# Token sums of a quartered product: from the head of the product phase into the normalisation loop, in a two-layer decoder step

## What is computed

```
h = rms_norm(x, norm_g[i])            # x: 1056 tokens x 1024
z = h @ W_in                          # 4096 columns (layer 0), 7168 (layer 1)
... pooling (layer 0) or stick-breaking attention (layer 1), memory attention ...
x = x + concat(branch * silu(gate), mem * silu(mgate)) @ w_out
```

## Time and profile before

| | us |
|---|---|
| median of 3 runs | 2482.71 (2480.73 to 2486.89) |
| the profiled execution | 2476.22 |
| its span, first to last instruction | 2474.5 |
| PE busy | 2229.4 (90%) |
| DVE, ACT, POOL busy | 1304.3, 1014.1, 451.2 |
| mean granted TensorE clock | 0.944 of full |

### The profile page before, as it was taken

One profiled execution on the slowest core, in us unless ns is written; L12 is line 12 of the kernel. 1 busy time (PEld: TensorE's weight loads), 2 busy tenths in 40 slices (PEclk: granted clock), 3 DMA queues, 4 the chain that ended last, 5 costly groups with the idle time before them and its releaser, 6 DMA issues. The chain is left out here.

```text
span 2474.5 us, 47020 instructions
## 1 busy us (share of the span) xinstructions
PE 2229.4 (90%) x18709; PEld 1857.7 (75%) x18709; DVE 1304.3 (53%) x2026; ACT 1014.1 (41%) x2096; POOL 451.2 (18%) x541
## 2 busy tenths in 40 slices
PE   4759999995899948999999997769999999997999
PEld 4659988885678738999999997756666666663787
DVE  5474765542531185434444442358888888774311
ACT  4334322222420053433332342336777777775200
POOL 0062321211100043222222220131111111010000
PEclk7879999997999959999999998789999999999999
DMA  5323222205453132333443332668999999987531
GB/s 187 128 66 102 63 74 75 83 20 215 147 169 102 51 119 83 108 105 119 144 130 96 105 104 112 204 238 309 388 409 407 394 396 391 390 313 266 165 102 51
DMA packets 260393, 441.18 MB, mean 178 GB/s; under 512 B 26067, under 2 KB 187295, under 8 KB 260159
## 3 DMA queue, kind: packets, MB, share of 16 engines
q1 hardware_dynamic: 252110, 408.81, 47.1%
q0 software_dynamic: 8064, 29.36, 3.1%
HBM read 367.85 MB, written 70.82 MB: 177 GB/s over the span
## 5 line engine op out<-in xcount | busy, mean ns | idle before, releaser
L232 DVE TENSOR_TENSOR h_w_lo<-l_w,h_w_hi 128x512 fp32r<-128x512 f32 x264 | 202.1, 767 | 218.7 <-ACT h_w_hi L225 216.4
L225 ACT ACTIVATE h_w_hi<-l_w 128x512 fp32r<-128x512 f32 x264 | 166.7, 632 | 218.4 <-PE i_c L296 76.0
L191 POOL TENSOR_TENSOR h_w_lo_full<-l_w 128x512 f32<-128x512 f32 x44 | 61.8, 1405 | 620.3 <-DMA l_w<-in_w_in_sb_dram 218.1
L294 PE MATMUL i_x<-h_t_hi,h_w_hi 128*128 128x264 f32 x560 | 162.9, 291 | 7.8 <-ACT i_stage L303 5.7
L294 PE MATMUL i_y<-h_t_hi,h_w_hi 128*128 128x264 f32 x560 | 162.1, 289 | 2.1 <-DVE h_t_lo L246 2.1
L2467 PEld LDWEIGHTS b_krow<-ar_arena,b_qd 128*32 128x32 f32 x3072 | 107.2, 111 | 72.6 <-issue 57.3
L296 PE MATMUL i_x<-h_t_hi,h_w_lo 128*128 128x264 f32 x560 | 160.6, 287 | 0.0
L295 PE MATMUL i_x<-h_t_lo,h_w_hi 128*128 128x264 f32 x560 | 160.0, 286 | 0.0
L295 PE MATMUL i_y<-h_t_lo,h_w_hi 128*128 128x264 f32 x560 | 159.8, 285 | 0.0
L296 PE MATMUL i_y<-h_t_hi,h_w_lo 128*128 128x264 f32 x560 | 159.6, 285 | 0.0
L2467 PE MATMUL b_krow<-ar_arena,b_qd 128*32 128x128 f32 x3072 | 140.7, 279 | 8.0 <-ACT b_kev L2173 6.6
(11 more groups left out here) (337 smaller groups left out, 6512.7 us busy)
## 6 DMA issues: line engine op xcount, KB each, us to landing
ar_arena<-in_cache_sb_k_dram SPq DMA_DIRECT2D x73, 768.0 KB, 9.6
bf_vpage<-in_cache_sb_v_dram SPq DMA_DIRECT2D x64, 768.0 KB, 9.0
b_vpage<-in_cache_sb_v_dram SPq DMA_DIRECT2D x64, 768.0 KB, 8.3
l_w<-in_w_in_sb_dram SPq DMA_DIRECT2D x56, 512.0 KB, 3.9
l_w<-in_cache_sb_k_dram SPq DMA_DIRECT2D x36, 768.0 KB, 9.8
...
```

The costliest lines, as they stand in the source:

```text
L191: gp.tensor_tensor(self.w_full[:, i % RING, :, :], a21, a22, ALU.add).then_inc(self.combined, 1)
L225: act.activation(self.w_hi[:, i % RING, :, :], self.source(i), ACT.Copy).then_inc(self.high, 1)
L232: dve.tensor_tensor(self.w_lo[:, i % RING, :, :], self.source(i), self.w_hi[:, i % RING, :, :].bitcast(F32), ALU.subtract).then_inc(self.r ...
L294: pe.matmul(out, w_hi, t_hi, start=kk == 0 and x in ("P1", "P2", "P5"), stop=False, skip_group_check=True)
```

## The change

The three full-width DVE sums and the one of POOL leave the head of the product phases. In the norm, behind the evacuation of each of tiles 4 to 8, DVE makes that tile's columns of sum 5 (`token_first`), waiting there for ACT's half of the evacuation. POOL makes sums 4, 3 and 6 in the same five column pieces (`token_sums`: 112, 3 x 128 and 32 columns, each 4 deep), in `norm_phase` behind its combines and in `front_phase` ahead of them.

```diff
+    def token_columns(self, t):
+        return slice(max(t * P - HALF, 0), t * P - HALF + (P if t < TILES else SAMPLES))
+
+    def token_first(self, dve, t):
+
+        b11, b12, t1 = (self.full[n][:, :, self.token_columns(t)] for n in (0, 3, 5))
+        dve.tensor_tensor(t1, b12, b11, ALU.subtract).then_inc(self.t_first, 1)
+
+    def token_sums(self, gp):
+
+        cols = [self.token_columns(t) for t in range(4, TILES + 1)]
+        for n, at in enumerate(cols):
+            gp.wait_ge(self.t_first, n + 1)
+            gp.tensor_tensor(self.full[4][:, :, at], self.full[2][:, :, at], self.full[5][:, :, at], ALU.subtract
+                             ).then_inc(self.t_added, 1)
+        for at in cols:
+            gp.tensor_tensor(self.full[3][:, :, at], self.full[2][:, :, at], self.full[3][:, :, at], ALU.subtract
+                             ).then_inc(self.t_added, 1)
+        gp.wait_ge(self.t_added, len(cols))
+        for at in cols:
+            gp.tensor_tensor(self.full[6][:, :, at], self.full[1][:, :, at], self.full[4][:, :, at], ALU.subtract
+                             ).then_inc(self.t_added, 1)
```

```diff
+    def token_high(self, act, t, cols=slice(0, HALF)):
+
+        if t == 5 and cols.start == 0:
+            act.wait_ge(self.t_first, TILES - 3)
+        if t in (4, 3, 6):
+            act.wait_ge(self.t_added, {4: 1, 3: 2, 6: 3}[t] * (TILES - 3))
+        act.activation(self.hi[t][:, :, cols], self.full[t][:, :, cols], ACT.Copy).then_inc(self.t_high, 1)
+
+    def token_rest(self, eng, t, n, signal, cols=slice(0, HALF)):
+
+        eng.wait_ge(self.t_high, n)
+        eng.tensor_tensor(self.lo[t][:, :, cols], self.full[t][:, :, cols], self.hi[t][:, :, cols].bitcast(F32), ALU.subtract
+                          ).then_inc(signal, 1)
+
+    def tokens_scalar(self, act, i):
+
+        if i == 0:
+            for n in range(2):
+                self.token_high(act, 5, slice(n * SUB, (n + 1) * SUB))
+        for t in {0: (0, 1), 1: (4,), 2: (2,), 3: (3,), 4: (6,)}.get(i, ()):
+            self.token_high(act, t)
+
+    def tokens_vector(self, dve, i):
+
+        if i == 0:
+            for n in range(2):
+                self.token_rest(dve, 5, n + 1, self.t_rest, slice(n * SUB, (n + 1) * SUB))
+        for t, n in {0: ((0, 3), (1, 4)), 1: ((4, 5),), 2: ((2, 6),)}.get(i, ()):
+            self.token_rest(dve, t, n, self.t_rest)
+
+    def tokens_gpsimd(self, gp, i):
+
+        for t, n in {3: ((3, 7),), 4: ((6, 8),)}.get(i, ()):
+            self.token_rest(gp, t, n, self.t_rest_g)
...
-        if p == 0:
-            pe.wait_ge(self.t_rest_g if x in ("P3", "P7", "P4") else self.t_rest,
-                       {"P5": 1, "P1": 2, "P2": 3, "P6": 4, "P3": 1, "P7": 2, "P4": 3}[x])
         t = self.TOKENS[x]
         for n in range(2):
+            if p == 0:
+                pe.wait_ge(self.t_rest_g if x in ("P7", "P4") else self.t_rest,
+                           {"P5": n + 1, "P1": 3, "P2": 4, "P6": 5, "P3": 6, "P7": 1, "P4": 2}[x])
```

P5 waits for each half of its operand by itself. The calls, in both product phases (here `pool_phase`, POOL and DVE; ACT has `q.tokens_scalar(act, 0)` and, at the end of its loop, `q.tokens_scalar(act, i + 1)`):

```diff
                 gp.memset(up[:, :, 0:HIST], 0.0).then_inc(s["zeroed"], 1)
-                q.tokens_gpsimd(gp)
                 for j in range(6, AHEAD + 1):
                     q.combine(gp, j)
                 for i, (p, x) in enumerate(q.seq):
+                    q.tokens_gpsimd(gp, i)
                     q.combine(gp, i + AHEAD + 1)
                     for n in range(GROUPS):
                         if (p, x) == (first(n), "P7"):
...
-                q.tokens_vector(dve)
+                q.tokens_vector(dve, 0)
                 for j in range(6, AHEAD):
                     q.remainder(dve, j)
                 for i, (p, x) in enumerate(q.seq):
...
+                    q.tokens_vector(dve, i + 1)
```

`Quads` allocates all seven token tiles at once, ahead of `front_phase`, and there the split memory weights lie in the ring of the token weights (slots 0 to 3 and 4 to 7); the first rounds wait until memory product 6 (`made` 14), and rounds 4 and 5 until product 7 (`made` 16):

```diff
-        w_hi = [k.sb(f"w_hi{n}", [P, KD, WC], F32R) for n in range(2)]
-        w_lo = [k.sb(f"w_lo{n}", [P, KD, WC], F32R) for n in range(2)]
+        w_hi, w_lo = ([ring[:, 4 * n:4 * n + 4, :, :].rearrange("p r k n -> p (r k n)").rearrange("p (k n) -> p k n", n=WC)
+                       for n in range(2)] for ring in (q.w_hi, q.w_lo))
...
-                 8: [("K", 1), ("P", 6), ("W", 7), ("X", 0), ("X", 3), ("P", 7), ("V", 1)]}
+                 8: [("K", 1), ("P", 6), ("W", 7), ("X", 0), ("P", 7), ("V", 1), ("X", 4)]}
...
+                q.token_sums(gp)
+                gp.wait_ge(s["made"], 14)
                 for j in range(6):
                     q.combine(gp, j)
...
-                            for j in range(n, n + 3):
+                            act.wait_ge(s["made"], 16 if n else 14)
+                            for j in range(n, min(n + 4, 6)):
                                 q.round(act, j)
```

More of the change, by code:

```diff
@@ L105, in __init__ @@
         self.full, self.lo = [], []
-        for n in range(4):
+        for n in range(7):
             self.allocate_tokens(n)
@@ L114, in __init__ @@
             k.sem(n) for n in ("loaded_a", "combined", "high", "rest", "done", "copied", "added"))
-        self.t_added, self.t_third, self.t_high, self.t_rest, self.t_rest_g = (
-            k.sem(n) for n in ("t_added", "t_third", "t_high", "t_rest", "t_rest_g"))
+        self.t_first, self.t_added, self.t_high, self.t_rest, self.t_rest_g = (
+            k.sem(n) for n in ("t_first", "t_added", "t_high", "t_rest", "t_rest_g"))
         self.seq = []
@@ L146, in allocate_rest @@
     def allocate_rest(self):
-        for n in range(4, 7):
-            self.allocate_tokens(n)
         self.hi = [self.k.sb(f"t_hi{n}", [P, K2, HALF], F32R) for n in range(7)]
@@ L233, in remainder @@
                           ALU.subtract).then_inc(self.rest, 1)
[L235 to L257, removed]
@@ L259, in tokens_gpsimd @@
-    def tokens_gpsimd(self, gp):
-        f = [t[:, :, :] for t in self.full]
-        gp.wait_ge(self.t_added, 1)
-        gp.tensor_tensor(f[3], f[2], f[3], ALU.subtract).then_inc(self.t_third, 1)
-        gp.wait_ge(self.t_added, 3)
-        gp.wait_ge(self.t_third, 1)
-        for n, t in enumerate((2, 3, 6)):
-            gp.wait_ge(self.t_high, n + 5)
-            gp.tensor_tensor(self.lo[t][:, :, :], f[t], self.hi[t][:, :, :].bitcast(F32), ALU.subtract
-                             ).then_inc(self.t_rest_g, 1)
+    def token_columns(self, t):
+        return slice(max(t * P - HALF, 0), t * P - HALF + (P if t < TILES else SAMPLES))
@@ L461, in evacuate @@
                     ins.then_inc(lo, 1)
+                    if t >= 4:
+                        dve.wait_ge(hi, t + 1)
+                        dve.wait_ge(lo, t + 1)
+                        q.token_first(dve, t)
                 for t in range(N):
@@ L672, in evacuate @@
                     ins.then_inc(s["lo"], 1)
+                    if t >= 4:
+                        dve.wait_ge(s["hi"], t + 1)
+                        dve.wait_ge(s["lo"], t + 1)
+                        q.token_first(dve, t)
                 def memory_norm(_):
@@ L939, in _ @@
                             begin(p + 1)
+                    q.tokens_scalar(act, i + 1)
             @block.vector
```

10 lines of the change are left out of this document (6 added, 4 removed).

## The result

| kernel | median of the runs, us | profiled execution, its span | mean clock |
|---|---|---|---|
| before | 2482.57 (2480.73 to 2486.89) | 2476.22, 2474.5 | 0.944 |
| changed | 2468.01 (2465.74 to 2469.42) | 2467.73, 2466.0 | 0.945 |

A forecast was written before the change was run, and what follows sets the result against it. PE, busy 90%, bounds the kernel; only its stands in the product phases can be won. Layer 0 -17.3 + 4.3, layer 1 -17.3 + 16.3, together -14.0 us: 2462.2 from the profile, 2468.7 from the median; range 2460 to 2479.

The forecast's parts named there:

- What bounds the phase: Product phases: PE stands waiting for DVE's lo and ACT's copies; reordering gains 17.3 us in each layer.
- one at a time: DVE and POOL two-input work: whoever starts second waits for the other's end; DVE's subtraction takes 1.17 instead of 0.69 us.
- The 4.7: Product phases: assumed time in us of one POOL lo tile working alone, never shown alone in the trace before.
- The clock at product 6: Product phases: after PE idles 4.3 us its clock falls, product 6 takes 4.6 us, product 7 starts at 34.1.
- the 51.4: Product phases: start of product 7 before the change, in us from the phase's first instruction; 34.1 forecast after.
- The norm: Layer 1's norm: DVE ends at 905.3, POOL's bare pieces last 12.3 us more; the phase ends 16.3 us later.
- 1.2 + 3 x 1.37 + 0.55: Layer 1's norm tail: time in us for POOL's five pieces of one sum, counted twice, for sums 3 and 6.
- The front: Layer 0's front phase: sums beside the memory products delay the values and the phase end by 4.3 us; bounds +1, +7.
- The sum: Whole kernel: -17.3 + 4.3 - 17.3 + 16.3 = -14.0 us; 2462.2 from the profiled execution, 2468.7 from the median.
- POOL's `lo` at 6.7 us: Rival, product phases: lo of 3 and 6 stay that long, so only -6 us in all, 2476.7; chance 0.14.
- long pieces: Rival, both phases with sums: POOL's pieces take 0.8 us more and cancel the gain, or reach 2503; chance 0.06.
- The fourth: Rival, behind the products: PE waits for something later anyway, so the gain is lost, about 2482.7; chance 0.06.

The follow-up runs named there:

- run 3: Kernel before with the token sums made early as in the full change, but the splitting in one block heading the product phases: 2486.92 us, ratio 1.0003.
- run 8: run 6 with sums 6 and 3 as whole VectorE tiles inside both layers' product phases: 2456.64 us, ratio 0.9875 to the kernel before.
- run 10: Kernel before once more, unchanged, for its trace: 316.9 us from layer 0's products to layer 1's norm; profiled execution 2476.1 us.
- run 6: Full change with lo of tokens 3 and 6 made by VectorE instead of GpSimd: 2459.15 us, ratio 0.9892 to the kernel before.

## Why the prediction was right

By its steps:

- **What bounds the phase, and one at a time**: right. First product 2.6 us into layer 1's phase (2.5 forecast), P6 at 13.4 (13.2), P7 at 22.4 (22.2), product 6 at 29.6 (29.5), product 7 at 34.8 (34.1). POOL's tile not started under another took 4.66 us (4.7). The 4.7 was a choice between 4.5 and 5.4 to 6.7, and run 3 and this trace bear it out.
- **The clock at product 6**: right in layer 1 (5.2 us for it, 4.6 forecast), not in layer 0. There P7, after an idle of 2.5 us, ran in part at the lower clock (4.5 us, granted 0.69), which the wait behind it hid, and product 6, after an idle of 2.8 us, took 3.1. So layer 0's product 7 came 32.7 us into the phase, 1.4 before the forecast; it had come at 52.3 before, 0.9 after the 51.4 that I took for both layers: 19.6 us gained, not 17.3.
- **The norm**: right in kind, 1.4 us too dear. DVE ended where it was said to (896.93, with the 8.5 us lead 905.4; forecast 905.3). The tail was 10.85, not 12.3: the term "1.2 + 3 x 1.37 + 0.55" for five pieces, 5.86, is 5.20 in the trace.
- **The front**: 4.2 us for 4.3, partly for another reason. I had memory product 6 end at 117.0 and POOL's sums at 118.2, and put the last 1.2 us on the sums; product 6 itself ended just before 118.33, and run 8 without sums 3 and 6 is no sooner. What was under-priced is the delay of the memory products, 3.2 us where I gave 2.0: PE waited 10.4 us for the keys instead of 8.5, where I gave +0.6. The total came out because the rest, rounds and values on ACT, was over-priced by as much; that is luck.
- **The sum**: -14.0 forecast, -17.0 by the traces up to the two products 7, -14.6 between medians and -16.4 by the ratio. The 3 us between forecast and traces are layer 0's phase (2.3) and the norm (1.4), less 0.8 in layer 1's phase, 16.5 gained there and not 17.3. Taking the terms from the trace but the level from the medians was what made the time right, and it was luck in part: by the spans of the two profiled executions the change brings 8.5 us, and from the profiled 2476.22 alone the forecast would have been 2462.2, below all four timed runs.
- **The rivals**: POOL's `lo` at 6.7 us did not come, nor long pieces (the pieces at 128x512 took 1.26). The fourth, gains that come to no use, did not come: there is no long wait of PE after product 7 in either layer. What the traces give back, 7 us in the memory attention, lies in code that is the same in both and goes with the granted clock (run 10).

What it had not seen is the size of what was left: VectorE and GpSimd take turns in two-input work, so a tile on GpSimd in a head costs about 4.7 us instead of 2.36 (run 6). That was its own premise; it was used to cost the change, not to ask what the change leaves. Nor did it ask what each half brings: by the ratios the interleaving alone gives -16.4, the sums alone +0.7, both together -16.4; by the traces -10.9, 0 and -17.0, so that the sums bring something only with the interleaving.
